# Feed-forward inputs: the last two column blocks transposed sooner, high parts of sums in a list of their own on ScalarE, and half blocks of the second layer squared by ScalarE

## What is computed

```python
# first block, after attention and retention
x = x + merged @ w_out[l]
h = rms_norm(x, norm_ffn[l])
x = x + (jax.nn.silu(h @ w_gate[l]) * (h @ w_up[l])) @ w_down[l]   # D_FF = 2816
# second block, after its attention and gating
x = x + rms_norm_2(mix, g_post_mix)
h = rms_norm_2(x, g_pre_ffn)
f = jnp.square(jax.nn.relu(h @ w_ff1)) @ w_ff2                     # D_FF_2 = 4096
return x + rms_norm_2(f, g_post_ffn)
```

## Time and profile before

| | us |
|---|---|
| median of 3 runs | 2594.77 (2594.12 to 2595.74) |
| the profiled execution | 2595.17 |
| its span, first to last instruction | 2593.3 |
| PE busy | 2550.8 (98%) |
| DVE busy | 1585.5 (61%) |
| POOL busy | 1246.0 (48%) |
| ACT busy | 1052.7 (41%) |

### The profile page before, as it was taken

The page is one execution under the profiler, slowest core; times in us unless marked ns, Lnnn a source line. Parts: engine busy times, 40 slices in busy tenths (PEclk is TensorE's granted clock), DMA queues, the critical chain, the costliest instruction groups (busy, mean ns, idle before and its releaser), DMA issues. The chain is left out here.

```text
span 2593.3 us, 35295 instructions
## 1 busy us (share of the span) xinstructions
PE 2550.8 (98%) x13038; PEld 2127.8 (82%) x13038; DVE 1585.5 (61%) x2592; ACT 1052.7 (41%) x2081; POOL 1246.0 (48%) x994
## 2 busy tenths in 40 slices
PE   8999999999999999999999999999998999999998
PEld 6888888677888888888888878998888888888886
DVE  7355554685536554454698761168658666587787
ACT  4332343584224332232444551169744322254443
POOL 2479784354525665555221774548545544200204
PEclk9999999999999999999999999999999999999999
DMA  5557674705551222222752344323143333364534
GB/s 216 193 185 284 223 263 155 276 18 190 187 184 66 74 89 90 79 77 72 284 191 94 110 151 180 89 65 86 51 132 106 114 106 112 118 250 134 184 102 166
DMA packets 162710, 372.40 MB, mean 144 GB/s; under 512 B 21538, under 2 KB 42658, under 8 KB 158882
## 3 DMA queue, kind: packets, MB, share of 16 engines
q1 hardware_dynamic: 162540, 370.15, 41.5%
HBM read 268.01 MB, written 101.83 MB: 143 GB/s over the span
## 5 line engine op out<-in xcount | busy, mean ns | idle before, releaser
L2353 POOL TENSOR_TENSOR WL<-WRAW,WH 128x512 fp32r<-128x512 f32 (+1 forms) x149 | 247.7, 1664 | 277.2 <-ACT WH L1098 277.1
L852 PE MATMUL PS<-HH,WL 128*128 128x512 f32 (+1 forms) x976 | 368.5, 378 | 2.6 <-DVE HL L1881 0.9
L854 PE MATMUL PS<-HL,WH 128*128 128x512 f32 (+1 forms) x976 | 366.7, 376 | 0.0
L855 PE MATMUL PS<-HH,WH 128*128 128x512 f32 (+1 forms) x976 | 366.6, 376 | 0.0
L1619 DVE TENSOR_TENSOR WL<-TS,WH 128x512 fp32r<-128x512 f32 x228 | 245.6, 1086 | 193.1 <-ACT WH L1098 193.0
L917 PE MATMUL PS<-WH,DAL 128*128 128x512 f32 x756 | 294.7, 390 | 0.0
L919 PE MATMUL PS<-WH,DAH 128*128 128x512 f32 x756 | 294.5, 390 | 0.0
L918 PE MATMUL PS<-WL,DAH 128*128 128x512 f32 x756 | 294.5, 390 | 0.0
L2532 POOL TENSOR_TENSOR X<-X,DV 128x512 f32<-128x512 f32 x56 | 90.1, 1633 | 354.4 <-DVE DV L2024 270.3
L1098 ACT ACTIVATE WH<-TS 128x512 fp32r<-128x512 f32 x228 | 138.3, 621 | 213.9 <-POOL TS L2369 213.8
L2369 POOL TENSOR_TENSOR TS<-WRAW 128x512 f32<-128x512 f32 x114 | 153.2, 1344 | 129.8 <-issue 122.6
(11 more groups left out here) (418 smaller groups left out, 6070.0 us busy)
## 6 DMA issues: line engine op xcount, KB each, us to landing
WRAW<-in_u_f SPq DMA_DIRECT2D x56, 512.0 KB, 3.9
WRAW<-in_u_in SPq DMA_DIRECT2D x54, 512.0 KB, 4.4
WRAW<-scr_t SPq DMA_DIRECT2D x52, 512.0 KB, 3.7
scr_h<-HS SPq DMA_DIRECT2D x96, 256.0 KB, 2.2
WRAW<-in_u_gu SPq DMA_DIRECT2D x44, 512.0 KB, 3.4
scr_t<-TTa SPq DMA_DIRECT2D x18, 1024.0 KB, 4.1
WRAW<-in_u_out SPq DMA_DIRECT2D x24, 512.0 KB, 3.5
scr_x<-X SPq DMA_DIRECT2D x24, 512.0 KB, 4.9
```

What stands on the lines that cost most here:

```text
L852: e.matmul(PS[:, b, 0:wd], wl[:, blk(kk)], op_moving(q, kk, c0, wd, 0), start=(kk == 0), stop=False)
L854: e.matmul(PS[:, b, 0:wd], wh[:, blk(kk)], op_moving(q, kk, c0, wd, 1), start=False, stop=False)
L855: mm = e.matmul(PS[:, b, 0:wd], wh[:, blk(kk)], op_moving(q, kk, c0, wd, 0), start=False, stop=(kk == 3))
L2353: e.tensor_tensor(lo, raw, hi.bitcast(F32), ALU.subtract).then_inc(*c.inc("w_lo_p", i))
```

## The change

Orders are changed in all queues, and the squares of the quarters done at P5, P4 and P3 go from DVE to ACT for blocks with m < 2 in layer 2. In PE's and ACT's queues the four turns of j = 2 now stand behind output 15, and those of j = 3 behind P2 (two), P4 and P3 of block (0,0); block (1,0) has none. ACT's high parts of sums leave `turn` and form a list `HIGH_TERMS` of their own: four behind outputs 8 and 10 each, four behind P1, one behind P4 and three behind P3 of (0,0). DVE has counts of its own (`SUMS_OUT`, `SUMS_PROD`): A21 and A22 of j = 2 behind output 15 (in layer 1 ahead of the norm of the last row, in layer 2 behind `whole_row` and the norm of row tile 3), A11 and A12 behind P1. `squared` is ACT's relu and square with a wait between them; the one for P5 stands behind P4 and the ones for P4 and P3 behind P3, after the turns, high parts and the split of the same step. SP's stores wait for them.

```diff
@@ -532,11 +532,16 @@
     for lay, nb in ((1, FF1), (2, FF2 // 2)):
         BLOCKS[lay] = [(0, 0, 256), (1, 0, 256), (0, 256, 256), (1, 256, 256)] + [(m, 0, 512) for m in range(2, nb)]
     BACKS = [(q, j) for j in range(4) for q in TURN]
-    AFTER_OUT = {7: 2, 8: 2, 9: 2, 10: 2}
-    AFTER_PROD = {0: [0, 1, 1, 1, 1, 0, 1], 1: [1, 1, 1, 0, 0, 0, 0]}
+    AFTER_OUT = {7: 2, 8: 2, 9: 2, 10: 2, 15: 4}
+    AFTER_PROD = {0: [0, 0, 0, 0, 2, 1, 1], 1: [0] * 7}
     LOW_TERMS = [(q, j) for j in range(4) for q in LOWS]
     LOW_OUT = {8: 1, 9: 3, 10: 1, 11: 3}
-    LOW_PROD = {0: [0, 0, 0, 1, 1, 1, 1], 1: [0, 1, 1, 1, 1, 0, 0]}
+    LOW_PROD = {0: [0, 0, 1, 1, 2, 0, 0], 1: [2, 2, 0, 0, 0, 0, 0]}
+    HIGH_TERMS = [(q, j) for j in range(4) for q in ("S1", "S3", "S2", "S4")]
+    HIGH_OUT = {8: 4, 10: 4}
+    HIGH_PROD = {0: [4, 0, 0, 0, 0, 1, 3], 1: [0] * 7}
+    SUMS_OUT = {**AFTER_OUT, 15: 2}
+    SUMS_PROD = {0: [2, 0, 0, 0, 2, 1, 1], 1: [0] * 7}
     LAG, LAG_SP = 4, 5
     EARLY_SUMS = [PAIR[lay, m] for lay in (1, 2) for m in (0, 1)]
     SUMS_AT = {1: {8: (0, (0, 1, 2, 3)), 12: (1, (0, 1)), 14: (1, (2, 3))},
@@ -1279,21 +1284,25 @@
                 e.activation(op_whole(q, j), ps, ACT.Copy).then_inc(*bk.free(key))
                 return
             e.activation(op_cols(q, j, 0), ps, ACT.Copy).then_inc(*c.inc("h_hi", key))
-            for sq in {"A22": (), "A11": ("S1",), "A12": ("S3", "S2", "S4")}[q]:
-                w.wait_ge(*c.at("s_ov", (k, j, sq)))
-                e.activation(op_cols(sq, j, 0), op_whole(sq, j), ACT.Copy).then_inc(*c.inc("h_hi", (k, sq, j)))
+
+        def high_terms(k, highs, n):
+            for _ in range(n):
+                q, j = highs.pop(0)
+                w.wait_ge(*c.at("s_ov", (k, j, q)))
+                e.activation(op_cols(q, j, 0), op_whole(q, j), ACT.Copy).then_inc(*c.inc("h_hi", (k, q, j)))
 
         def turns(k, backs, n):
             for _ in range(n):
                 turn(k, *backs.pop(0))
 
-        backs = list(BACKS)
+        backs, highs = list(BACKS), list(HIGH_TERMS)
         for i, (nh, tt) in enumerate(OUTS):
             if i in COMPLETE:
                 w.wait_ge(*bk.out(("out", 0, tt)))
                 w.wait_ge(*bk.out(("out", 1, tt)))
                 square(2, tt, SS[0][:, tt:tt + 1])
             turns(2, backs, AFTER_OUT.get(i, 0))
+            high_terms(2, highs, HIGH_OUT.get(i, 0))
             if i < 15:
                 feed(("out", nh, tt))
 
@@ -1314,7 +1323,15 @@
                 e.activation(half_slot(WH, op), d_weights(lay, n, i), ACT.Copy).then_inc(*c.inc("w_hi", op))
                 n_split[0] = op + 1
 
-        def strassen(lay, k, fn, backs, also=None):
+        def squared(m, c0, wd, p):
+
+            t = quarter(2, m, DONE[p])[:, c0:c0 + wd]
+            w.wait_ge(*bk.out((p, 2, m, c0)))
+            e.activation(t, t, ACT.Relu).then_inc(*c.inc("f_r", (m, c0, p)))
+            w.wait_ge(*c.at("f_r", (m, c0, p)))
+            e.activation(t, t, ACT.Square).then_inc(*c.inc("f_s", (m, c0, p)))
+
+        def strassen(lay, k, fn, backs, highs, also=None):
             for m, c0, wd in BLOCKS[lay]:
                 cs = slice(c0, c0 + wd)
                 gate, up = lay == 1 and m % 2 == 0, lay == 1 and m % 2 == 1
@@ -1340,14 +1357,16 @@
                         w.wait_ge(*bk.out(key))
                         e.activation(t, t, fn).then_inc(*c.inc("g_s", key))
                     elif lay == 2 and p == "P2":
-                        w.wait_ge(*bk.out(key))
-                        e.activation(q11, q11, fn).then_inc(*c.inc("f_r", (m, c0)))
-                        w.wait_ge(*c.at("f_r", (m, c0)))
-                        e.activation(q11, q11, ACT.Square).then_inc(*c.inc("f_s", (m, c0)))
+                        squared(m, c0, wd, "P2")
                     if c0 == 0 and m in AFTER_PROD:
                         turns(k, backs, AFTER_PROD[m][x])
+                        high_terms(k, highs, HIGH_PROD[m][x])
                         if m == 0:
                             split()
+                    if lay == 2 and m < 2 and p in ("P4", "P3"):
+                        squared(m, c0, wd, "P5" if p == "P4" else "P4")
+                        if p == "P3":
+                            squared(m, c0, wd, "P3")
                     if BEHIND[key][0] and (m, c0) != (0, 0):
                         feed(BEHIND[key][0])
                     if (m, c0, wd) == BLOCKS[lay][-1] and p == "P5":
@@ -1408,7 +1427,7 @@
             if s - 1 in range(4):
                 square_g(tt - 1)
 
-        strassen(1, 2, ACT.Silu, backs)
+        strassen(1, 2, ACT.Silu, backs, highs)
         ffn_down(1, fin1)
 
         def zu(j, half):
@@ -1587,6 +1606,7 @@
                 e.activation(X[:, tt, hs(nh)], PS[:, bk.at(key), :], ACT.Square,
                              accum_out=SS[2][:, tt:tt + 1]).then_inc(*c.inc("n_sq", (50, tt)))
             turns(4, backs, AFTER_OUT.get(i, 0))
+            high_terms(4, highs, HIGH_OUT.get(i, 0))
             if i < 15:
                 feed(key)
 
@@ -1600,7 +1620,7 @@
                 w.wait_ge(*c.at("n_sq", (6, tt - 1)))
             square(6, tt, SS[1][:, tt:tt + 1], SQ[:, :])
 
-        strassen(2, 4, ACT.Relu, backs, lambda: front3(PO[7]))
+        strassen(2, 4, ACT.Relu, backs, highs, lambda: front3(PO[7]))
         ffn_down(2, fin2)
         for s in range(4):
             fin2(1, s)
@@ -1891,10 +1911,13 @@
             w.wait_ge(*c.at(f"x{tt}", 2))
             e.tensor_tensor(X[:, tt, hs(nh)], PS[:, bk.at(key), :], X[:, tt, hs(nh)],
                             ALU.add).then_inc(*bk.free(key))
+            if i == 15:
+                turns(2, backs, SUMS_OUT[i])
             if i in COMPLETE:
                 w.wait_ge(*c.at("gb0", 2))
                 norm(2, tt, GF[:, :])
-            turns(2, backs, AFTER_OUT.get(i, 0))
+            if i < 15:
+                turns(2, backs, SUMS_OUT.get(i, 0))
             if i < 15:
                 feed(key)
 
@@ -1974,15 +1997,15 @@
                         w.wait_ge(*bk.full(key))
                         w.wait_ge(*c.at("b_y", ("P5", lay, m, c0)))
                         e.tensor_tensor(q12, ps, q12, ALU.add).then_inc(*bk.free(key))
-                    if lay == 2 and p in ("P5", "P4", "P3"):
+                    if lay == 2 and m >= 2 and p in ("P5", "P4", "P3"):
                         t = quarter(2, m, DONE[p])[:, cs]
                         w.wait_ge(*bk.out(key))
                         e.scalar_tensor_tensor(out=t, in0=t, scalar=0.0, in1=t, op0=ALU.max,
                                                op1=ALU.mult).then_inc(*c.inc("f_m2", (m, c0, DONE[p])))
                     if c0 == 0 and m in AFTER_PROD:
-                        turns(k, backs, AFTER_PROD[m][x])
                         if also and m == 0:
                             also(x)
+                        turns(k, backs, SUMS_PROD[m][x])
                         if m == 0:
                             if not on_pool(n_split[0]):
                                 split(n_split[0])
@@ -2286,7 +2309,7 @@
                 second_norm(OUTS[i - 1][1])
             if i in COMPLETE:
                 variance(4, tt, SS[0], VV[0])
-            turns(4, backs, AFTER_OUT.get(i, 0))
+            turns(4, backs, SUMS_OUT.get(i, 0))
             if i < 15:
                 feed(("o2", nh, tt))
 
@@ -2959,7 +2982,7 @@
                         if lay == 1:
                             w.wait_ge(*c.at("f_m", (m, c0, qq)))
                         else:
-                            w.wait_ge(*(c.at("f_s", (m, c0)) if p == "P2" else c.at("f_m2", (m, c0, qq))))
+                            w.wait_ge(*(c.at("f_s", (m, c0, p)) if p == "P2" or m < 2 else c.at("f_m2", (m, c0, qq))))
                         f, t0 = 2 * (m // 2 if lay == 1 else m) + (qq[1] == "2"), 512 * (qq[0] == "2") + c0
                         e.dma_start(scr_h[lay][f][:, t0:t0 + wd], quarter(lay, m, qq)[:, c0:c0 + wd]).then_inc(
                             *c.inc(f"h{qq}_{c0 // 256}", (lay, m, c0), 16))
```

## The result

The changed kernel takes **2601.7 us** (median of 10 executions, 2597.7 to 2605.0), the kernel before beside it 2594.4 (10 executions, 2593.3 to 2595.7). The ratio is 1.0027, 95% interval [1.0018, 1.0035]: 7.3 us slower, where the forecast was 2600.9. Its profiled execution, 2605.03 us, is the longest of the ten, with a span of 2602.9.

A forecast was written before the change was run, and what follows sets the result against it. PE is busy 98% of the span, so only its idle time can be won. Layers lose 2.8 + 3.3 = 6.1 us; profiled 2595.17 becomes 2601.3, median 0.4 lower: 2600.9 us, 8-in-10 range 2593.5 to 2604.5.

The forecast's parts named there:

- The sum: Entrances of both feed-forward layers: 2.8 us later in the first and 3.3 in the second, 6.1 us in all.
- signs asked for: Both entrances: PE idle some 3 us, clock near 0.5, P6's add at 12 us, lengths 52.1 and 57.6; B22 under 27.5 wrong.
- the half clock, counted once: Second layer's entrance: half clock for 3.4 us behind the idle 3.1 us makes the work behind 1.7 us later.
- 5 us late. From there each product of (0,0) costs an exchange: First layer: pair 0's B22 split and P6's add come 5 us late, then exchanges follow; P6 of (0,256) 2.8 us later.
- The walk: Four queues replayed with measured prices; old order's first full-width product at 873.9 and 2012.0, trace 873.78 and 2011.64.
- the delay that the prediction told from the idle stretch on: Second layer: PE idles 3.1 us, P6 and P7 sums 3.5 us late, then row 7 and the chain; 1.6 us without half clock.
- The later fall, at the turns of j=3: Second layer: a clock fall at the 2.8 us gap before j=3's first turn is absorbed by waits behind it.
- The stores behind these squares, whose cover the prediction argued: SP's queue, second layer: stores wait for ACT's squares, weight fetches land 5 us later, covered by 14 products, 20 us.
- Clock stays up: Rival, second layer: no half clock behind the idle entrance; 4.4 us slower, 2599.2 us; chance 0.25.
- Falls in the first layer too: Rival: half clock also behind gaps before P2 and P4 of (1,0), 1.7 us more, 2602.6 us; chance 0.13.
- Freed squares carry the second layer: Rival: DVE rid of its squares, second layer comes out even; 2.8 us remain, 2597.6 us; chance 0.12.
- Faster: Rival: j=3 operands earlier, (0,256) follows (1,0) without wait, B22 in time; each layer wins 2.5 us, 2589.8; chance 0.10.

The follow-up runs named there:

- j=2 only: Kernel before with only the first layer's turns, sums and low parts of j=2 at their new places, no list of high parts: 2595.0 us, ratio 0.9999.
- j=3 only: Kernel before with only the first layer's turns, sums and low parts of j=3 at their new places, no list of high parts: 2598.3 us, ratio 1.0012.
- j=3 undone: Changed kernel with turns, sums, high and low parts of j=3 back at their old places in both layers: 2596.5 us, ratio 1.0007.
- the filled kernel: Changed kernel with identity transposes for PE ahead of the second layer's first turn (28) and layer 1's P2 (16) and P4 (20) of (1,0): 2602.6 us.
- order only: Changed kernel with the squares back on DVE: 2604.8 us, ratio 1.0039 to the kernel before.
- the filled entrance: Changed kernel with 24 identity transposes for PE ahead of the second layer's first turn, none in the first layer: 2600.3 us, ratio 1.0021.
- squares only: Kernel before, old order, with only the layer 2 squares of the change moved from DVE to ACT: 2593.6 us, ratio 0.9995.
- the two filled kernels: Changed kernel with identity transposes ahead of the second layer's first turn; one also has them ahead of layer 1's P2 and P4: 2600.3 and 2602.6 us.
- layer 1 only: Kernel before with the new order and ACT's list of high parts in the first layer only: 2597.5 us, ratio 1.0011.
- splits first: Kernel before with ACT's squares, and pair 1's weight splits ahead of each step's turns, sums and low parts in blocks (0,0): 2590.1 us, ratio 0.9981.

## Why the prediction was right, and where it was not

**The sum held, +6.1 us forecast, +7.3 measured**, and so did all of the signs asked for. It held in part by luck: the reasons given for the delays were only partly right in either layer, and the half clock, counted once, came and went from one execution to the next. P6's add in the first layer starts 11.7 us after the outputs (12 forecast, 6.9 before), B22 of pair 1 is split 29.9 us after them (the bound was 27.5), PE idles 3.15 us ahead of the second layer's first turn (3.1) with half clock behind, and the entrances grew by 3.55 and 3.8 (2.8 and 3.3).

**The reason given for the first layer's delay was wrong.** The step "5 us late. From there each product of (0,0) costs an exchange" traced the loss back to the four turns of j=2 ahead of row 7's norm. "j=2 only" has just this delay: its split of pair 0's B22 ends 12.0 us after the outputs, 7.0 before. But by B22 of pair 1 nothing of it is left (24.9 against 25.0): the splits catch up step by step, 5.0, 4.1, 2.9, 0.9 and -0.2 us late. With j=2 done early there are no turns behind P6, P7, P5 and P2, which leaves DVE and ACT the room. What isn't caught up are the turns of j=3 in the last steps of (0,0): "j=3 only" has the whole loss, "j=3 undone" has none in this layer. The walk had this in it; asked for the two parts, it gives +0.2 and +2.4 (measured -0.4 and +2.9). I had read the story off one walk with everything changed, and told the delay in the order of time as if the first late instruction were the cause.

**A term was missing in the first layer: the clock.** I gave a fall around the waits of 2.0 and 2.3 us 0.13; it is in all five traces with this layer and no fill. The six traces with this order give its price (the sixth is the filled kernel):

| half clock in the first entrance, us | 0 (filled) | 3.4 | 6.8 | 10.2 |
|---|---|---|---|---|
| entrance, us | 51.7 | 51.7 | 52.7, 52.9, 52.9 | 54.1 |

Without half clock it is +2.4 (2.8 forecast), and 6.8 us of it add 1.0 to 1.2; 3.4 us, all ahead of P4, add nothing. The way is in the timeline: P4 of (1,0) starts at 854.71 and at half clock takes until 857.4, while B22, on which P3 waits, is ready at 856.25. The rule of the Trainium skill, "TensorE: Matmul & The Clock Gate", Part 1, that the clock follows how busy the engine has been of late, speaks for giving this case more weight than I did; the windows at 0.50 behind the gaps agree with it. The length of the one gap before doesn't decide it: the idle 3.0 us of "order only" and "j=3 undone" had no half clock right behind. The spread of the changed kernel's ten executions goes the same way: the three with a mean clock of 0.995 took 2604.5 to 2605.0, the three with 0.998 took 2597.7 to 2599.8. That ties the spread to the clock; that the clock is its only cause isn't shown, as the filled kernel's median says.

**In the second layer** the sizes stood up, the reason only in part. +3.3 was forecast, +3.8 is in the trace; the filled entrance, without half clock there, has +2.2 (1.6 forecast), so where the fall comes it costs 1.6 (1.7 forecast). It comes in one of the three traces that have this idle stretch unfilled (the changed kernel, "order only", "j=3 undone"). And the delay that the prediction told from the idle stretch on (P6 and P7 late, row 7 late, then the whole chain) is worth 0.9 us of the 2.2 by the trace of "j=3 undone", where the turns of j=3 stand where they were; the other 1.3 goes with them, as in the first layer. The later fall, at the turns of j=3, was held to cost nothing, and 3.4 or 6.8 us of it make the same entrance in the two filled kernels. The squares: 1.8 us by the trace of "squares only" (2.2 by the walk), 2.4 in the traces of "order only" and the changed kernel, 2.7 in their medians. The 0.42 us of an undisturbed square on DVE, which the rows beside that number don't show, is in the trace of before, for five of the eleven squares. The stores behind these squares, whose cover the prediction argued, were not tested by themselves.

**The rivals.** *Clock stays up*: in the profiled execution it doesn't; the filled kernel's trace gives its entrances +4.6 (4.4). *Falls in the first layer too*: true of the profiled execution. It gave 2602.6, the forecast 2600.9, and the measured 2601.7 lies as near to the one as to the other, so the time doesn't choose between them. *Freed squares carry the second layer*: no, they pay about 2 us of what the order costs. *Faster*: (0,256) does follow (1,0) without a wait, but B22 comes 4.9 us late, not in time.

## What to carry to other kernels

Where queues take turns in an exchange, don't blame the first instruction that is late: move one group at a time in the walk, and see whether the delay is still there at the instruction that ends last. Here that was the split of the next weights, and preparing an operand of the next block (j=3) sooner put it behind; the gain lay in the opposite, turns later or splits sooner, in the first layer down to 0.7 us above PE's own work. A right sum over a walk doesn't prove the story told about it. A wait of 2 us on PE can cost more than its length: here 6.8 us at half clock behind it made the entrance 1.0 to 1.2 us longer, and 3.4 us made it no longer.

## What the hardware showed that was not expected

Inside the work of the fourteen traced executions half clock came in stretches of 3.4, 6.8 and 10.2 us. It didn't come behind each gap. Six traces have the same idle 2.26 us in the second layer: "before" and "j=3 only" had half clock right behind it, "squares only", "layer 1 only", "j=2 only" and "splits first" had not. The idle 3.0 us at the second entrance brought it once in three, the wait of 2.0 us before P2 in the first layer each of the six times that it stands unfilled. The same first layer had 3.4, 6.8 and 10.2 us of it in different executions. Such a kernel's time may also spread more: 7.4 us for the changed kernel, 2.5 for the one before, over ten executions each. That is not shown to be a rule: "splits first", with no half clock in its trace, spreads over 7.1 us by one execution that stands alone.
